# ScalarE copies one item's turned probabilities before it takes the next item's exponential

## The reference

```
x: (1, 512, 1024), DEPTH = 2 layers
def hybrid_layer(x, ...):
    proj = rms_norm(x, norm_g) @ w_in + b_in          # 50 column blocks of 128, and 24 of gates
    y_a = indexer_sparse_attention(a_q, a_k, a_v, ...)   # 8 heads, top 128 keys of 512
    y_b = chunked_relpos_attention(b_q, b_k, b_v, ...)   # 8 heads, band of keys, relative bias
    y_c = mlstm_chunkwise(c_q, c_k, c_v, c_i, c_f, c_o)  # 4 heads
    merged = sum of sigmoid(gates) * (branch * silu(z)) @ w_branch
    return x + merged @ w_out
# within a and b, for each head and each block of 128 queries:
#   s = q k^T * scale (+ bias), masked;  p = softmax(s);  o = p v
```

## Time and profile before

| | |
|---|---|
| median of 3 runs | 1399.68 us (1398.15 to 1401.8) |
| the profiled execution | 1404.01 us, its span 1402.2 us |
| PE busy | 1314.3 us, 94% of the span |
| DVE busy | 768.9 us, 55% |
| ACT busy | 623.5 us, 44% |
| POOL busy | 482.2 us, 34% |
| granted PE clock, mean | 0.974 |

### The profile page before, as it was taken

The page is one execution under the profiler, slowest core; times in us unless marked ns, Lnnn a source line. Parts: engine busy times, 40 slices in busy tenths (PEclk is TensorE's granted clock), DMA queues, the critical chain, the costliest instruction groups (busy, mean ns, idle before and its releaser), DMA issues.

```text
span 1402.2 us, 20000 instructions
## 1 busy us (share of the span) xinstructions
PE 1314.3 (94%) x6525; PEld 1094.7 (78%) x6525; DVE 768.9 (55%) x1444; ACT 623.5 (44%) x1119; POOL 482.2 (34%) x227
## 2 busy tenths in 40 slices
PE   5997999999998999999999799898999989999997
PEld 3786787778887788888878677786889868888886
DVE  5688787776456311212868887778554551112166
ACT  4443555757543333323344356465755343323332
POOL 2542322222223344444554232222212234444451
PEclk8998999999999999999999899999999999999999
DMA  6221211121122223333242131112212213233231
GB/s 232 84 90 61 91 61 46 53 68 61 61 92 82 68 83 107 92 100 112 66 177 91 60 105 61 46 51 63 68 46 106 76 43 107 90 97 97 92 103 60
DMA packets 37034, 117.42 MB, mean 84 GB/s; under 512 B 4064, under 2 KB 6496, under 8 KB 36448
## 3 DMA queue, kind: packets, MB, share of 16 engines
q1 hardware_dynamic: 34368, 111.37, 24.1%
q10 hardware_dynamic: 2592, 5.11, 1.2%
HBM read 110.18 MB, written 6.29 MB: 83 GB/s over the span
## 4 chain that ended last, share of the span: by engine, by line
PE 69%; DVE 20%; issue 5%; ACT 3%; POOL 1%; DVEq 0%; DMA 0%; ACTq 0%; SPq 0%; POOLq 0%
PE acc L574 56%; PE ps_o L683 3%; DVE score L1160 3%; DVE top L1158 2%; PE ps_t L670 2%; PE ps_t L661 1%; PE ps_o L690 1%; DVE prob L1198 1%; DVE bk_lo_s L1150 1%; PE ps_s L640 1%; DVE turn L1174 1%; DVE att_c L1299 1%; PE spare L700 1%; DVE turn L1097 1%; DVE aq_s L1138 1%
## 5 line engine op out<-in xcount | busy, mean ns | idle before, releaser
L524 POOL TENSOR_TENSOR w_lo<-w_raw,w_hi 128x1024 fp32r<-128x1024 f32 (+1 forms) x212 | 470.0, 2218 | 886.8 <-ACT w_hi L765 886.8
L574 PE MATMUL acc<-h_hi,w_hi 128*128 128x512 f32 x1136 | 459.3, 404 | 16.8 <-ACT w_hi L765 16.8
L574 PE MATMUL acc<-h_lo,w_hi 128*128 128x512 f32 x1136 | 450.1, 396 | 0.0
L574 PE MATMUL acc<-h_hi,w_lo 128*128 128x512 f32 x1136 | 301.3, 400 | 1.3 <-POOL w_lo L524 1.3
L574 PEld LDWEIGHTS acc<-h_hi,w_hi 128*128 128x128 f32 x1136 | 216.6, 191 | 58.9 <-ACT w_hi L765 18.1
L765 ACT ACTIVATE w_hi<-w_raw 128x1024 fp32r<-128x1024 f32 (+1 forms) x212 | 203.9, 962 | 129.9 <-PE acc L574 99.8
L574 PEld LDWEIGHTS acc<-h_lo,w_hi 128*128 128x128 f32 x1136 | 216.4, 191 | 40.5
L574 PEld LDWEIGHTS acc<-h_hi,w_lo 128*128 128x128 f32 x1136 | 211.3, 191 | 43.7 <-POOL w_lo L524 2.1
L1312 DVE SCALAR_TENSOR_TENSOR gated<-prob,acc 128x512 f32<-128x512 f32 x16 | 11.0, 687 | 251.8 <-PE acc L574 251.8
L965 ACT ACTIVATE prob<-acc,par_half 128x512 f32<-128x512 f32 x48 | 33.1, 690 | 154.4 <-PE acc L574 154.4
L915 ACT ACTIVATE prob<-prob,neg_max 128x128 f32<-128x128 f32 (+3 forms) x128 | 70.9, 554 | 56.1 <-DVE neg_max L1198 55.8
(11 more groups left out here) (239 smaller groups left out, 1887.6 us busy)
## 6 DMA issues: line engine op xcount, KB each, us to landing
w_raw<-w_full SPq DMA_DIRECT2D x164, 512.0 KB, 3.4
w_raw<-w_mix SPq DMA_DIRECT2D x48, 256.0 KB, 2.6
x_kept<-xT SPq DMA_DIRECT2D x2, 2048.0 KB, 9.3
rel<-rel ACTq DMA_DIRECT2D x16, 256.0 KB, 2.7
xT<-x_kept SPq DMA_DIRECT2D x2, 2048.0 KB, 9.5
stage<-x SPq DMA_DIRECT2D x4, 512.0 KB, 7.2
out<-stage SPq DMA_DIRECT2D x4, 512.0 KB, 2.9
consts<-consts ACTq DMA_DIRECT2D x1, 640.0 KB, 4.4
```

The costliest lines, as they stand in the source:

```text
L524: pool.tensor_tensor(w_lo[:, slot, 0:nk, :], w_raw[:, raw, 0:nk, :], w_hi[:, slot, 0:nk, :].bitcast(F32), ALU.subtract).then_inc(split_ful ...
L574: last = pe.matmul(acc[slot][:, :], w[:, slot, k, :], x[:, k, :], start=(i == 0), stop=(i == 3 * nk - 1))
```

## The change

Each place of items a and b lists `turn_p` of item n-2 ahead of `exp` of item n-1. PE has no instruction for the step `exp`, and DVE has none for `exp` or, for items a and b, for `turn_p`; their lists stay the same row for row. POOL's and SP's too. Only ACT takes its two instructions in the other order.

```diff
         mlstm = any(m is not None and m >= 64 for m in flying[-4:])
-        for back, kind in ((1, "exp"), (2, "turn_p"), (3, "values")) if mlstm else ((2, "exp"), (3, "turn_p"), (4, "values")):
+        for back, kind in ((1, "exp"), (2, "turn_p"), (3, "values")) if mlstm else ((3, "turn_p"), (2, "exp"), (4, "values")):
             if len(flying) >= back and flying[-back] is not None:
                 seq.append((kind, flying[-back]))
```

## The result

| | before | after |
|---|---|---|
| median | 1399.68 us (1398.15 to 1401.8) | 1407.83 us (1404.85 to 1410.57) |
| ratio | | 1.0059, 95% interval 1.0045 to 1.0074 |
| the profiled execution, its span | 1404.01, 1402.2 us | 1410.57, 1408.7 us |
| granted PE clock, mean | 0.974 | 0.975 |

The change makes the kernel 0.6% slower, 8.2 us by the medians, where 4.3 were forecast. The time lies in the range of 1398 to 1410; the likeliest class of change, within 0.3%, did not come true, but the next, slower, did. It lies 1.1 us above A's own range, which ended at 1406.7, and at the lower edge of C's, +8 to +11 us.

The account below looks back on a forecast made before the run. PE sets the time and waits for ACT's exponential, not the copy. Later turns cost 2.47 us in the first layer and 1.87 in the second, 4.3 in all: 1399.7 + 4.3 = 1404.0 us, range 1398 to 1410.

Parts of the forecast that it names:

- A: The forecast itself: PE's persistent waits for exponentials grow, +4.3 us, within +2.5 and +7; chance 0.50.
- C: Clock rival: longer PE pauses bring two or three more dips to half clock, +8 to +11 us; chance 0.15.
- turn(43): PE's turn for item 43, already waiting; copy(42) goes ahead of its exponential: +0.37 us in each layer.
- turn(51): PE's turn for item 51, already waiting; copy(50) goes ahead of its exponential: +0.37 us in each layer.
- turn(54): PE's turn for item 54, already waiting; copy(53), 0.36 us, goes ahead: +0.26 us in each layer.
- turn(57) of the first layer: PE's turn for item 57: exp(55) and `ya_hi` come later, delaying DVE and exp(57): +0.86 us.
- turn(60): PE's turn for item 60; copy(59), 0.57 us, goes ahead: +0.47 us per layer, a new wait.
- turn(63): PE's turn for item 63, where the pipeline drains; copy(62) delays its exponential: +0.40 us in each layer.
- turn(57) of the second layer: PE's turn for item 57, which did not wait in the old trace: only 0.26 us later.
- The turns left out: Six turns of items 33, 39, 20, 21: at most 0.37 us each, 2.2 in all, swallowed by PE's pauses for DVE.
- as nothing says which way the hits go: POOL delaying DVE's `bk_lo`: spared hits would make the sum 0.9 us, new ones as much more; 4.3 kept.
- The claims on the two doors: PE's pauses for DVE, 4.31 us before values(20) in the second layer and 1.69 before scores(44), should shrink a little.

Follow-up runs that it names:

- late_only: Kernel before with the exchange only in seven places of each layer (exponentials of items 43, 51, 54, 55, 57, 60, 63): 1403.43 us, ratio 1.0020.
- not_late: Kernel before with the exchange everywhere but in the places of exponentials 43, 51, 54, 55, 57, 60, 63: 1400.47 us, ratio 0.9998.
- before_dve_first: Kernel before, with POOL waiting where the second layer begins until DVE's last `xg_lo` is done: 1398.47 us, ratio 0.9988.
- a_only: Kernel before with the exchange only in places whose exponential belongs to branch a (items below 32): 1399.88 us, ratio 0.9994.
- the two shifted kernels: Branch-b-only exchange and full change, each with first-layer score matmuls of item 42 made twice, 43 three times: 1403.80 us (1.0033) and 1407.31 us (1.0057).
- b_only: Kernel before with the exchange only in places whose exponential belongs to branch b (items 32 to 63): 1403.62 us, ratio 1.0019.
- b_only_shift: Kernel before with the exchange for items 32 to 63, plus first-layer score matmuls of item 42 made twice, 43 three times: 1403.80 us, ratio 1.0033.
- after_again: The changed kernel measured once more, nothing else altered, against the kernel before: 1407.11 us, ratio 1.0052.
- w_hi_last: Kernel before with ACT's `w_hi` copy moved behind the following pair of exponential and copy, without the exchange: 1398.00 us, ratio 0.9982.

## Why the prediction was right and wrong

- *The direction and the mechanism* were right: PE waits for the exponential, not for the copy, and pays where it is at the turn first. `late_only` and `not_late` show it by time, for less than half of the loss.
- *The terms, one by one.* Forecast and measured in us: turn(43) 0.37, 0.42; turn(51) 0.37, 0.37; turn(54) 0.26, 0.24 to 0.26; turn(57) of the first layer, its chain over `ya_hi` included, 0.86, 0.95 where no dip hides it; turn(60) 0.47, a wait of 0.54 that was not there; turn(63) 0.40, a wait of 0.23, but only 0.1 later against turn(60). For turn(57) of the second layer the prediction had 0.26, as it did not wait in the trace; but that execution had the dip there. `before_dve_first`, without it, has a wait of 0.66 us, and `late_only` and the full exchange 1.36 to 1.38, so this term is some 0.7 us too small. This lack and the excess of turn(63), 0.3 us in each layer, nearly cancel, and the sum of 4.3 us comes out: `late_only` falls behind `before_dve_first` by 2.3 us from turn(20) to turn(63) of the first layer and by 2.4 of the second, 4.6 in all. It costs only 0.20%, 2.8 us, since some is taken back between: it has one half-clock stretch at 450 us where the other has two (granted clock 0.83 and 0.66 from 450 to 460).
- *The turns left out* (33, 39, 20, 21): that they grow (2.4 us for 2.2, of which turn(33) has 0.6 to 0.7 in each layer where 0.37 was to be the most) and are swallowed is shown by `a_only`, `not_late` and the two shifted kernels.
- *What failed* is the step from the sum to the time: rival C was held apart from A, with a chance of 0.15, though the two came together. The range was met by the room that it left for C; and a change in the number of dips or of hits on `bk_lo` was one of the prediction's own signs of being wrong, and it came. The longer pause before turn(54) came with a dip of the clock in all four profiles of the full exchange, 1.7 us. And "as nothing says which way the hits go" put the hit of POOL on `bk_lo` at nothing: the dip brings one, 1.25 us of waiting. The Trainium skill, SBUF — State Buffer, section "SBUF: two separate sides", has the engine that starts first hold the shared ports for a whole instruction. The rows agree: POOL 0.02 us ahead, 3.62 us for DVE's pair, against 1.39 in `late_only`, where DVE began first. The extras are not worth their sum, 1.7 + 1.25 less the 0.70 us by which turn(57) then need not wait longer, 2.25 us; the table shows 1.5 on top of the exchange. With that the sum is 4.6 + 1.5 = 6.1 us, an estimate from the profiles.
- *What stays open.* How much is left to explain beyond the 6.1: the change measured 8.2, 6.5 and 7.0 us between the medians of three groups, with intervals that overlap. And why 57 harmless items bring the package to the seven. The gap between the parts and the whole is in large part the clock: over all runs the mean granted clock is 0.9780 to 0.9784 in `late_only`, `b_only`, `not_late` and `b_only_shift`, 0.9772 in `a_only`, 0.9773 to 0.9775 in the three groups of the kernel before, and 0.9759 to 0.9764 in the four groups of the full exchange. By estimate that is 0.0021 x 1400 = 3 us between the parts and the whole, and 2 us between before and the whole; it is an upper figure, since half clock costs time only where PE sets it. The kernel before has the package in some executions too, in the second layer, among them but not `before_dve_first`; that may be why its runs spread over 1395 to 1404 us, and was only argued. `late_only` has the same pause of 1.16 us before turn(54) and neither. The Trainium skill, TensorE: Matmul & The Clock Gate, section "Part 1: The HAM clock gate", ties the clock to how busy PE was; that fits a dip behind a pause, but not by itself that the same pause has one in one kernel and none in another. The pause stands some tenths of a microsecond elsewhere; the kernels that should have moved it did not.
- The claims on the two doors were half right: the 4.31 us became 4.21, but the 1.69 us became 1.75, since POOL was first at that `bk_lo` too.

## What to carry to other kernels

When one engine makes two things for another, keep them in the order in which they are used, and look for the price first where the user is already waiting: seven places of 64 held what the sum counted. Read such waits from more than one execution: a dip of the clock hid one of them (turn(57)) in the only trace that the prediction had. Ask of each what the longer pause may do to the clock, and whether a shift brings an instruction of POOL ahead of one of DVE that it then holds up. It is the same for a wait removed: 4.5 us less on ACT's side came with POOL's `w_lo` ahead of another instruction of DVE (2.44 us for 0.55) and with a lower mean clock, and 2.3 us were left.

## What the hardware showed that I had not expected

- DVE's `xg_lo` took 0.75 us when it began 0.05 us ahead of POOL's `w_lo` in `after_again`, and 2.95 us in the first profile of the change, where it began 0.05 us ahead too. The start shown does not tell who has the port; only the durations do (POOL 2.94 us, then 2.36).
- PE's pause before turn(54) of the first layer was followed by 3.4 us at half clock in four of four executions of the full exchange and in none of seven others with a pause of 0.9 or 1.2 us there.
- DVE's L1171, a TENSOR_SCALAR of 128x512, took 2.44 us in `w_hi_last` where POOL's `w_lo` began 0.22 us ahead of it, and 0.55 us in the kernel before.
- 1.25 us of added matmuls ahead of a door of DVE's cannot be told from nothing: 1403.80 for 1403.62 us and 1407.31 for 1407.11, with ratios of 1.0033 for 1.0019 and 1.0057 for 1.0052, the intervals overlapping.
